# Norm borders of a fused transformer kernel: last tile in token halves, matmuls of the high parts first, one combined sum for the double norm

## The chip, the cores and the metric

The kernel runs on one core of one Trainium2 chip, as one program without collectives. The metric is the device time of an execution in microseconds; the median of several executions is given. About 0.3% (6 us) is what such a measurement can tell from no change.

## What is computed

One sequence of T = 512 tokens and D = 1024 features passes through two layers of a first block (an HGRN and stick-breaking mixer, then a gated mLSTM-like mixer, each followed by a convolutional gated feed-forward), a norm, one layer of a second block (dilated and top-k sparse attention, then a gated feed-forward) and a last norm. What matters here stands between the stages:

```python
def rmsnorm(x, g):
    return x * lax.rsqrt(jnp.mean(x * x, axis=-1, keepdims=True) + EPS) * g

x = x + gate * (y @ w_out)                       # residual
h = rmsnorm(x, g) * (1.0 + scale) + shift        # input of the next stage
```

`gate`, `scale` and `shift` come from a modulation `silu(c) @ ada_w + ada_b`. Between the blocks x is normed twice: x = rmsnorm(x, final_g), then rmsnorm(x, g_attn) enters the second block. The product of the first norm is also the residual stream of the second block.

## The kernel before

All data is kept features on partitions: X is `[128, 8, 512]`, eight tiles of 128 features by 512 tokens (KT = 8). Weights stream from DRAM in 302 chunks of 128x1024 through two buffers (SyncE issues the DMAs). For precision each chunk is split by GpSimd into a high part (L429) and a low part (L431, `w_lo = raw - w_hi`) of type fp32r, in four slots; the split of chunk n waits until TensorE has finished chunk n-4 (`pe_done`, the tiny operation L428). Activations are split in the same way: ScalarE writes `Hhi`, VectorE writes `Hlo`. A matmul block is then three matmuls of 128x512 in fp32r (`three`, L446 to L449): high by high, weight high by activation low, weight low by activation high. One chunk is one output tile: `tile_chunk` (L451) runs k = 0 to 7 with three matmuls each, 24 in all, into one of four PSUM banks G[0..3].

The stages (PHASES, L63) follow each other: even_in, even_out, ffn0, down0, odd_in, odd_out, ffn1, down1, idx_in, attn_in, attn_out, ffn2, down2. Each engine has its own hand-written program; they meet in counting semaphores. VectorE also works through the 144 chunks of the modulation (L1080), and ScalarE issues a few small loads in its own queue.

The first tiles of a stage that follows a norm are run k by k over two output chunks at once (`first_tiles`, L479; three in odd_out, four in even_in), so that TensorE can begin when the first k is there. It waits for `h_ready`, which VectorE raises when the low part is written.

A **norm border** lies between two stages, at r = 1 (behind even_out), 2 (down0), 3 (odd_out), 4 (down1, the double one), 5 (attn_out) and 6 (down2, the end). Its steps, for the last tile m = 7:

1. VectorE adds the residual from PSUM (`residual`, L1098).
2. ScalarE squares the tile (L1724). The squares of the seven tiles before are already added up in `sq_acc` by VectorE (L1365).
3. TensorE sums both over the features, a product with a column of ones per block of 128 tokens (`partial_sums`, L533; each is a pair of loads and matmuls, 8 for a tile), into `normps`.
4. ScalarE takes the root (L1729, in the double and last border L2046), VectorE the reciprocal (L1114). VectorE has meanwhile made the gain column `acol` (L1133).
5. TensorE spreads the 512 values over all partitions, four blocks of 128 tokens (`token_rows`, L555, L558), into `rstdps`.
6. VectorE scales tile k with gain and root (`scaled`, L1151) into `work`; ScalarE adds the shift and writes `Hhi` (L1738); VectorE writes `Hlo` (`low`, L1158).
7. TensorE starts `first_tiles`.

Between these steps TensorE runs dummy matmuls (`keep_warm`, L528, L531) whose results nobody reads: WARM[0] = 2 before the last tile's sums, 1 behind them (3 in the double border), WARM[2] = 4 behind the broadcast. Each is two passes of 256 columns.

In the double border VectorE and ScalarE make a second square of every tile, times `final_g` (L1903), summed in a second accumulator; after the first reciprocal VectorE computes the mean square of the normed x (L1142 to L1144), ScalarE takes a second root (L2051), VectorE a second reciprocal and a product (L1146, L1147). A second broadcast, of the first norm's root, follows the first tiles (L921). In the last border (`normed_x`, L1344) VectorE scales X itself, tile by tile, and SyncE writes each tile out.

## Time and profile before

| | |
|---|---|
| median of 3 runs | 1991.24 us (1988.09 to 1993.24) |
| profiled execution, its own time | 1991.48 us |
| its span, first to last instruction | 1989.7 us |
| TensorE matmul busy | 1923.1 us (97%) |
| TensorE weight load busy | 1551.2 us (78%) |
| VectorE, ScalarE, GpSimd busy | 1034.7, 451.9, 1184.4 us |
| mean granted TensorE clock | 0.985 of full |
| DMA | 242.23 MB, 122 GB/s mean |
| chain that ended last | 86% TensorE, 7% VectorE, 3% ScalarE |

A matmul's own duration in the profile (392 ns in the mean for 128x512) contains its passage through the array; back to back they start 0.23 us apart, so the busy share counts overlapping work once. Idle time of an engine costs only where another engine waits for it.

### The profile page before, as it was taken

Reading aid. Unit: us, or ns where it says so; the run is one execution under the profiler, and the core shown is the slowest. Engines: PE = TensorE matmul, PEld = TensorE weight load, DVE = VectorE, ACT = ScalarE, POOL = GpSimd, SP = SyncE. Lnnn points to the kernel's source line nnn. Section 1 sums busy time; section 2 is a strip of 40 time slices with the busy share of each in tenths; the row PEclk is TensorE's granted clock in tenths of the full one; section 3 lists DMA queues with packets and bytes.
Section 4 is the critical chain, followed back from the end, with each engine's and each line's share of the span. In section 5 each row is a group of like instructions: output and inputs, shape, how many; then the busy total and the mean of one; then the engine's idle time right before and its main releaser. Section 6 shows DMA issues by size and latency. Waiting matters only on the chain.

```text
span 1989.7 us, 25330 instructions
## 1 busy us (share of the span) xinstructions
PE 1923.1 (97%) x8824; PEld 1551.2 (78%) x8824; DVE 1034.7 (52%) x1529; ACT 451.9 (23%) x774; POOL 1184.4 (60%) x907
## 2 busy tenths in 40 slices
PE   5999999999999999999999999999988899999998
PEld 4787868888888887667788888887766688888886
DVE  7566256666655453466766663233877453323222
ACT  3302342211210022352221211112228421111100
POOL 3743326788887955324688787746540256666773
PEclk7999999999999999999999999999989999999999
DMA  7432223455554422111455553322210023222332
GB/s 305 177 117 75 96 95 106 170 190 192 204 193 174 172 96 85 53 52 55 157 191 193 197 189 117 105 96 85 74 59 17 27 82 104 95 95 95 106 105 74
DMA packets 67375, 242.23 MB, mean 122 GB/s; under 512 B 7498, under 2 KB 7882, under 8 KB 67314
## 3 DMA queue, kind: packets, MB, share of 16 engines
q1 hardware_dynamic: 65536, 237.01, 34.2%
q10 hardware_dynamic: 1778, 4.37, 0.6%
q8 instruction: 43, 0.70, 0.1%
q14 instruction: 18, 0.15, 0.0%
HBM read 239.25 MB, written 2.10 MB: 121 GB/s over the span
## 4 chain that ended last, share of the span: by engine, by line
PE 86%; DVE 7%; ACT 3%; issue 2%; DMA 2%; POOL 1%; DVEq 0%; SPq 0%; ACTq 0%; POOLq 0%
PE gemm L447 23%; PE gemm L448 23%; PE gemm L449 23%; DMA w_raw<-wstream 2%; DVE b_score L1630 1%; PE mix L650 1%; PE gemm L474 1%; PE gemm L476 1%; PE gemm L475 1%; DVE b_top L1625 1%; PE mix L447 1%; PE gemm L1046 1%; PE gemm L803 1%; DVE sq_acc L1365 1%; PE mix L449 1%
## 5 line engine op out<-in xcount | busy, mean ns | idle before, releaser
L431 POOL TENSOR_TENSOR w_lo<-w_raw,w_hi 128x1024 fp32r<-128x1024 f32 x302 | 734.9, 2433 | 25.2
L447 PE MATMUL gemm<-h_hi,w_hi 128*128 128x512 f32 x1616 | 634.0, 392 | 20.8 <-DVE h_lo L1186 14.6
L448 PE MATMUL gemm<-h_lo,w_hi 128*128 128x512 f32 x1616 | 630.1, 390 | 0.0
L449 PE MATMUL gemm<-h_hi,w_lo 128*128 128x512 f32 x1616 | 630.1, 390 | 0.0
L428 POOL TENSOR_TENSOR pool_gate<-pool_gate 128x1 f32<-128x1 f32 x298 | 118.3, 397 | 734.4 <-PE gemm L449 592.8
L447 PEld LDWEIGHTS gemm<-h_hi,w_hi 128*128 128x128 f32 x1616 | 304.2, 188 | 90.2 <-issue 21.8
L429 POOL TENSOR_SCALAR w_hi<-w_raw 128x1024 fp32r<-128x1024 f32 x302 | 344.1, 1139 | 17.5 <-DMA w_raw<-wstream 17.5
L449 PEld LDWEIGHTS gemm<-h_hi,w_lo 128*128 128x128 f32 x1616 | 304.0, 188 | 63.8
L448 PEld LDWEIGHTS gemm<-h_lo,w_hi 128*128 128x128 f32 x1616 | 304.1, 188 | 62.0
L1080 DVE CUSTOM_DVE_ANT_0 ada_raw<-ada_raw,c_act 128x1024 f32<-128x1024 f32 x128 | 216.5, 1707 | 110.1 <-DMA ada_raw<-adastream 110.1
L449 PE MATMUL gemm<-p_hi,w_lo 128*128 128x512 f32 x528 | 205.4, 389 | 0.0
L447 PE MATMUL gemm<-p_hi,w_hi 128*128 128x512 f32 x528 | 205.4, 389 | 0.0
L448 PE MATMUL gemm<-p_lo,w_hi 128*128 128x512 f32 x528 | 205.4, 389 | 0.0
L1098 DVE SCALAR_TENSOR_TENSOR x_res<-gemm,modv,x_res 128x512 f32<-128x512 f32 x48 | 35.9, 747 | 238.7 <-PE gemm L449 238.7
L1393 DVE TENSOR_TENSOR work<-work,gemm 128x512 f32<-128x512 f32 x66 | 45.4, 688 | 176.5 <-PE gemm L449 140.3
L1395 DVE TENSOR_TENSOR p_lo<-work,p_hi 128x512 f32 x66 | 98.6, 1494 | 61.4 <-ACT p_hi L1927 61.4
L1724 ACT ACTIVATE sq_tile<-x_res 128x512 f32 x48 | 30.3, 632 | 430.4 <-DVE x_res L1098 430.4
L1365 DVE TENSOR_TENSOR sq_acc<-sq_acc,sq_tile 128x512 f32<-128x512 f32 x42 | 98.6, 2348 | 36.7 <-ACT sq_tile L1724 36.7
L449 PEld LDWEIGHTS gemm<-p_hi,w_lo 128*128 128x128 f32 x528 | 99.1, 188 | 20.8
L448 PEld LDWEIGHTS gemm<-p_lo,w_hi 128*128 128x128 f32 x528 | 99.1, 188 | 20.6
L447 PEld LDWEIGHTS gemm<-p_hi,w_hi 128*128 128x128 f32 x528 | 99.1, 188 | 20.4
L1921 ACT ACTIVATE work<-work 128x512 f32<-128x512 f32 x44 | 27.8, 633 | 307.1 <-DVE work L1388 307.1
(339 smaller groups left out, 1972.0 us busy)
## 6 DMA issues: line engine op xcount, KB each, us to landing
w_raw<-wstream SPq DMA_DIRECT2D x302, 512.0 KB, 3.5
ada_raw<-adastream SPq DMA_DIRECT2D x128, 512.0 KB, 4.3
a_early<-adastream SPq DMA_DIRECT2D x8, 1024.0 KB, 11.9
out<-x_res SPq DMA_DIRECT2D x8, 256.0 KB, 2.2
c_act<-c_in ACTq DMA_DIRECT2D x2, 512.0 KB, 7.2
x_res<-x_in SPq DMA_DIRECT2D x2, 512.0 KB, 6.3
x_res<-x_in ACTq DMA_DIRECT2D x2, 512.0 KB, 9.0
b_dist<-const_in ACTq DMA_DIRECT2D x1, 512.0 KB
```

What stands on the lines that cost most here:

```text
L428: pool.tensor_tensor(pgate[:], pgate[:], pgate[:], ALU.mult)
L429: pool.tensor_scalar(whi[s][:], raw[:, u % RAW, :], 1.0, 0.0, ALU.mult, ALU.add).then_inc(w_hi_done, 1)
L431: pool.tensor_tensor(wlo[s][:], raw[:, u % RAW, :], whi[s][:].bitcast(F32), ALU.subtract).then_inc(w_split, 1)
L447: pe.matmul(out_ap, w_h, r_h, start=first, stop=False)
L448: pe.matmul(out_ap, w_h, r_l, start=False, stop=False)
L449: return pe.matmul(out_ap, w_l, r_h, start=False, stop=last)
L1080: dve.tensor_tensor_reduce(w, w, c, 1.0, start, ALU.mult, ALU.add, total).then_inc(ada_used, 1)
L1098: dve.scalar_tensor_tensor(out=X[:, ds(m, 1), :].rearrange("p a t -> p (a t)"), in0=G[bank][:], scalar=modv[:, ds(gate + m, 1)], in1=X[:, ...
L1365: dve.tensor_tensor(sqacc[:], sqacc[:], sqt[:, m % 2, :], ALU.add).then_inc(sq_added, 1)
L1393: dve.tensor_tensor(work[:, 2 + jj, :], y, G[2 * jj + 1][:], ALU.mult).then_inc(gfree[2 * jj + 1], 1)
L1395: dve.tensor_tensor(Plo[:, ds(2 * i + jj, 1), :].rearrange("p a t -> p (a t)"), work[:, 2 + jj, :], Phi[:, ds(2 * i + jj, 1), :].rearrange ...
L1724: act.activation(sqt[:, slot, :], X[:, ds(m, 1), :].rearrange("p a t -> p (a t)"), ACT.Square).then_inc(sq_ready, 1)
```

## The change

- `first_tiles` waits for the high part of k only, runs the two matmuls of each output tile that use it, and then the low matmuls of k-1; the low matmuls of k = 7 come last. It is used in all nine stages of FILL (L348).
- The last residual, its square and its column sums are made in two halves of 256 tokens. The first two blocks of the root are broadcast into M[0], then blocks 2, 3, 0, 1 into `rstdps` (12 instructions instead of 8); the first tile of `work` and of `Hhi` is made in two halves, the first from M[0].
- The dummies are WARM[0] = 1 before the last sums, WARM[1] = 2 behind them, WARM[2] = 3 behind the broadcast (into M[1]; none in the double border).
- The double norm uses one sum: for gain g the squares are taken with the scale sqrt(g*g + eps) and the root with the bias eps*eps, so that the reciprocal is the product of both norms' factors. The plain sum of the last tile comes behind the broadcast, its root and reciprocal behind the last low part.
- `squares` on ScalarE is unrolled instead of a loop. Columns of `acol` hold the new gains and eps*eps; four semaphores are new (`last_half`, `sq_half`, `bc_half`, `t_half`). No tile is added.

The diff, indented less, without those names, `HALF = T // 2` and some context:

```diff
@@ -74,7 +74,7 @@
...
 ADA_SLOTS = 4
-WARM = (2, 4, 4, 14)
+WARM = (1, 2, 3, 14)
@@ -478,20 +485,31 @@
     def first_tiles(phase, fill, count=2, before={}):
+        def low(k):
+            pe.wait_ge(h_ready, KT * fill + k + 1)
+            for u in range(count):
+                s = (N0[phase] + u) % SPL
+                mm = pe.matmul(G[u][:], whi[s][:, k * P:(k + 1) * P], Hlo[:, k, :], start=False, stop=(k == KT - 1))
+                if k == KT - 1:
+                    mm.then_inc(pe_done, 1)
         for u in range(count):
...
                 before[k]()
-            pe.wait_ge(h_ready, KT * fill + k + 1)
+            w = slice(k * P, (k + 1) * P)
+            pe.wait_ge(hhi_ready, KT * fill + k + 1)
             for u in range(count):
...
                 s = (N0[phase] + u) % SPL
-                mm = three(G[u][:], whi[s][:, k * P:(k + 1) * P], wlo[s][:, k * P:(k + 1) * P],
-                           Hhi[:, k, :], Hlo[:, k, :], k == 0, k == KT - 1)
-                if k == KT - 1:
-                    mm.then_inc(pe_done, 1)
+                pe.matmul(G[u][:], whi[s][:, w], Hhi[:, k, :], start=(k == 0), stop=False)
+                pe.matmul(G[u][:], wlo[s][:, w], Hhi[:, k, :], start=False, stop=False)
+            if k:
+                low(k - 1)
+        low(KT - 1)
     def tiles(phase, bodies, done=0, wide=2):
@@ -525,36 +543,43 @@
...
-    def keep_warm(n):
+    def keep_warm(n, bank=M[0]):
         for _ in range(n):
-            pe.matmul(M[0][:, 0:256], const("ones"), cst[:, 0:256], start=True, stop=True)
-    def partial_sums(c0, tile, first, last):
-        for j in range(NTB):
+            pe.matmul(bank[:, 0:256], const("ones"), cst[:, 0:256], start=True, stop=True)
+    borders = [0]
+    def partial_sums(c0, tile, first, last, blocks=range(NTB)):
+        for j in blocks:
             mm = pe.matmul(normps[:, c0 + j:c0 + j + 1], tile[:, j * P:(j + 1) * P], const("ones")[:, 0:1],
...
     def norm_scale(r):
+        borders[0] += 1
         pe.wait_ge(sq_added, KT * r + KT - 1)
         partial_sums(0, sqacc, True, False)
-        keep_warm(WARM[0])
-        pe.wait_ge(sq_ready, KT * (r + 1))
-        mm = partial_sums(0, sqt[:, 1, :], False, True)
+        c0, last = 0, sqt[:, 1, :]
         if r == 4:
             pe.wait_ge(gsq_added, KT)
-            partial_sums(4, work[:, 2, :], False, False)
+            c0, last = 8, work[:, 1, :]
+            partial_sums(c0, work[:, 2, :], False, False)
+        keep_warm(WARM[0])
+        pe.wait_ge(sq_half, borders[0])
+        partial_sums(c0, last, False, True, (0, 1))
+        if r == 4:
             pe.wait_ge(gsq_ready, KT)
-            mm = partial_sums(4, work[:, 1, :], False, True)
-        mm.then_inc(norm_sum, 1)
-        keep_warm(3 if r == 4 else 1)
-    def token_rows(ps, c0):
-        for j in range(NTB):
+        else:
+            pe.wait_ge(sq_ready, KT * (r + 1))
+        partial_sums(c0, last, False, True, (2, 3)).then_inc(norm_sum, 1)
+        keep_warm(WARM[1])
+    def token_rows(ps, c0, blocks=range(NTB)):
+        for j in blocks:
             mm = pe.matmul(ps[:, j * P:(j + 1) * P], rst[:, c0 + j:c0 + j + 1].broadcast_to([P, P]), const("ident"),
@@ -567,10 +592,16 @@
     def norm(r):
         norm_scale(r)
+        c0 = 8 if r == 4 else 0
         bc[0] += 1
-        bcast(rstdps, bc[0])
-        if r not in (0, 6):
-            keep_warm(WARM[2])
+        pe.wait_ge(rstd_ready, bc[0])
+        token_rows(M[0], c0, (0, 1)).then_inc(bc_half, 1)
+        token_rows(rstdps, c0, (2, 3, 0, 1)).then_inc(rstd_bc, 1)
+        if r == 4:
+            pe.wait_ge(sq_ready, KT * (r + 1))
+            partial_sums(0, sqt[:, 1, :], False, True).then_inc(norm_sum, 1)
+        elif r != 6:
+            keep_warm(WARM[2], M[1])
@@ -583,7 +614,7 @@
...
     bcast(rstdps, bc[0])
-    keep_warm(WARM[2])
+    keep_warm(4)
     def stick_z(h):
@@ -910,11 +941,7 @@
...
-    norm_scale(4)
-    bc[0] += 1
-    bcast(rstdps, bc[0] + 1, 8)
-    keep_warm(WARM[2])
+    norm(4)
     first_tiles("idx_in", FILL["idx_in"])
@@ -1098,15 +1125,12 @@
...
-    def add_square(r, m, slot, first):
-        dve.wait_ge(sq_ready, m + KT * r + 1)
-        if first:
-            ins = dve.tensor_copy(sqacc[:], sqt[:, slot, :])
-        else:
-            dve.wait_ge(sq_added, m + KT * r)
-            ins = dve.tensor_tensor(sqacc[:], sqacc[:], sqt[:, slot, :], ALU.add)
-        ins.then_inc(sq_added, 1)
+    def last_residual(n, m, bank, gate):
+        dve.wait_ge(pe_done, n + 1)
+        for half, done in ((slice(0, HALF), last_half), (slice(HALF, T), gfree[bank])):
+            dve.scalar_tensor_tensor(out=X[:, m, half], in0=G[bank][:, half], scalar=modv[:, gate + m:gate + m + 1],
+                                     in1=X[:, m, half], op0=ALU.mult, op1=ALU.add).then_inc(done, 1)
     def inverse_rms(n, src):
@@ -1124,32 +1148,29 @@
...
     rms_n = [0]
+    borders = [0]
+    def border_inverses(c0):
+        borders[0] += 1
+        rms_n[0] += 1
+        dve.wait_ge(rms_ready, rms_n[0])
+        ready(dve.reciprocal(rst[:, c0:c0 + 4], rms[:, c0:c0 + 4]))
+        dve.wait_ge(bc_half, borders[0])
     def norm(r, fill, g, shift_scale, first_gain=None):
-        rms_n[0] += 1
         a = acol[:, 8 * r:8 * r + 8]
...
                                       op0=ALU.add, op1=ALU.mult))
-        if first_gain is None:
-            ready(inverse_rms(4, rms_n[0]))
-        else:
-            ready(inverse_rms(4, rms_n[0]))
-            dve.wait_ge(rstd_ready, inverses_done[0])
-            rms_n[0] += 1
+        if first_gain is not None:
             link(dve.tensor_tensor(a, a, first_gain, ALU.mult))
-            link(dve.tensor_tensor(rst[:, 4:8], rst[:, 0:4], rst[:, 0:4], ALU.mult))
-            dve.tensor_tensor(rst[:, 4:8], rst[:, 4:8], normps[:, 4:8], ALU.mult).then_inc(sig("second_mean"), 1)
-            dve.wait_ge(rms_ready, rms_n[0])
-            link(dve.reciprocal(rst[:, 8:12], rms[:, 8:12]))
-            ready(dve.tensor_tensor(rst[:, 8:12], rst[:, 8:12], rst[:, 0:4], ALU.mult))
-        spread()
-        def scaled(k):
-            dve.scalar_tensor_tensor(out=work[:, k % 4, :], in0=X[:, k, :], scalar=a[:, k:k + 1], in1=rstdps[:],
-                                     op0=ALU.mult, op1=ALU.mult).then_inc(t_ready, 1)
+        border_inverses(0 if first_gain is None else 8)
+        def scaled(k, part=slice(0, T), done=t_ready, bank=rstdps):
+            dve.scalar_tensor_tensor(out=work[:, k % 4, part], in0=X[:, k, part], scalar=a[:, k:k + 1], in1=bank[:, part],
+                                     op0=ALU.mult, op1=ALU.mult).then_inc(done, 1)
         def low(k):
@@ -1158,18 +1179,24 @@
...
-        scaled(0)
+        scaled(0, slice(0, HALF), t_half, M[0])
+        spread()
+        scaled(0, slice(HALF, T))
         scaled(1)
...
                 scaled(k + 2)
+        if first_gain is not None:
+            rms_n[0] += 1
+            ready(inverse_rms(4, rms_n[0]))
...
     dve.memset(sqacc[:], 1.0).then_inc(sig("ones_set"), 1)
+    dve.memset(eps_sq, EPS * EPS).then_inc(sig("eps_sq_set"), 1)
     dve.memset(modsum[:], 0.0).then_inc(mod_added, 1)
     def first_modulation(k):
@@ -1344,20 +1371,24 @@
     def normed_x(r, g, bank=rstdps, done=False):
         if not done:
-            rms_n[0] += 1
-            ready(inverse_rms(4, rms_n[0]))
+            border_inverses(0)
+            dve.scalar_tensor_tensor(out=X[:, 0, 0:HALF], in0=X[:, 0, 0:HALF], scalar=g[:, 0:1], in1=M[0][:, 0:HALF],
+                                     op0=ALU.mult, op1=ALU.mult)
         spread()
-        for k in range(KT):
+        if not done:
+            dve.scalar_tensor_tensor(out=X[:, 0, HALF:T], in0=X[:, 0, HALF:T], scalar=g[:, 0:1], in1=bank[:, HALF:T],
+                                     op0=ALU.mult, op1=ALU.mult).then_inc(sig("x_normed"), 1)
+        for k in range(0 if done else 1, KT):
             dve.scalar_tensor_tensor(out=X[:, k, :], in0=X[:, k, :], scalar=g[:, k:k + 1], in1=bank[:],
...
     def residual_tiles(phase, r, gate):
         dve.wait_ge(mod_added, gate // 4 - 1)
-        for m in range(KT):
+        for m in range(KT - 1):
             residual(N0[phase] + m, m, m % 4, gate)
-            if m < KT - 1:
-                add_square_prev(r, m)
+            add_square_prev(r, m)
+        last_residual(N0[phase] + KT - 1, KT - 1, 3, gate)
     def add_square_prev(r, m):
@@ -1409,9 +1440,11 @@
...
             for m in range(4):
-                residual(12 * i + N0[phase] + 3 * m + 2, 4 * i + m, m, gate)
                 if 4 * i + m < KT - 1:
+                    residual(12 * i + N0[phase] + 3 * m + 2, 4 * i + m, m, gate)
                     add_square_prev(r, 4 * i + m)
+                else:
+                    last_residual(12 * i + N0[phase] + 3 * m + 2, 4 * i + m, m, gate)
                 if group is not None and 1 <= 4 * i + m <= 4:
@@ -1719,20 +1752,26 @@
...
     scaled = [0]
-    def square(m, slot):
-        act.activation(sqt[:, slot, :], X[:, ds(m, 1), :].rearrange("p a t -> p (a t)"), ACT.Square).then_inc(sq_ready, 1)
-    def norm(r, fill, shift, table=None):
+    borders = [0]
+    def roots(c0, bias):
         nrm[0] += 1
         act.wait_ge(norm_sum, nrm[0])
-        act.activation(rms[:, 0:4], normps[:, 0:4], ACT.Sqrt, bias=col("eps"), scale=1.0 / D).then_inc(rms_ready, 1)
+        act.activation(rms[:, c0:c0 + 4], normps[:, c0:c0 + 4], ACT.Sqrt, bias=bias, scale=1.0 / D).then_inc(rms_ready, 1)
+    def norm(r, fill, shift, table=None):
+        roots(0, col("eps"))
         if table is not None:
...
     def high_tiles(shift):
-        for k in range(KT):
+        act.wait_ge(t_half, borders[0])
+        act.activation(Hhi[:, 0, 0:HALF], work[:, 0, 0:HALF], ACT.Identity, bias=modv[:, shift:shift + 1])
+        act.wait_ge(t_ready, scaled[0] + 1)
+        act.activation(Hhi[:, 0, HALF:T], work[:, 0, HALF:T], ACT.Identity, bias=modv[:, shift:shift + 1]).then_inc(hhi_ready, 1)
+        for k in range(1, KT):
@@ -1892,16 +1931,29 @@
     def squares(r, phase, gain=None):
         act.preload_act_table(ACT.Sqrt)
-        with act.Fori(0, 2) as i:
-            for u in range(4):
-                act.wait_ge(gfree[u], i + G0[phase][u] + 1)
-                act.wait_ge(sq_added, 4 * i + KT * r + u - 1)
-                square(4 * i + u, u % 2)
-                if gain is not None:
-                    act.wait_ge(gsq_added, 4 * i + u + 1)
-                    act.activation(work[:, u % 2, :], X[:, ds(4 * i + u, 1), :].rearrange("p a t -> p (a t)"), ACT.Square,
-                                   scale=cols[:, ds(4 * i + gain + u, 1)]).then_inc(gsq_ready, 1)
+        if gain is not None:
+            link(act.activation(gain, col("final_g", 0, 8), ACT.Square))
+            link(act.activation(gain, gain, ACT.Sqrt, bias=col("eps")))
+        for m in range(KT - 1):
+            act.wait_ge(gfree[m % 4], m // 4 + G0[phase][m % 4] + 1)
+            act.wait_ge(sq_added, KT * r + m - 1)
+            act.activation(sqt[:, m % 2, :], X[:, m, :], ACT.Square).then_inc(sq_ready, 1)
+            if gain is not None:
+                act.wait_ge(gsq_added, m + 1)
+                act.activation(work[:, m % 2, :], X[:, m, :], ACT.Square, scale=gain[:, m:m + 1]).then_inc(gsq_ready, 1)
+        m = KT - 1
+        borders[0] += 1
+        act.wait_ge(sq_added, KT * r + m - 1)
+        if gain is not None:
+            act.wait_ge(gsq_added, m + 1)
+        for half, there, count, done in ((slice(0, HALF), last_half, borders[0], sq_half),
+                                         (slice(HALF, T), gfree[3], G0[phase][3] + 2, sq_ready if gain is None else gsq_ready)):
+            act.wait_ge(there, count)
+            if gain is None:
+                act.activation(sqt[:, 1, half], X[:, m, half], ACT.Square).then_inc(done, 1)
+            else:
+                act.activation(work[:, 1, half], X[:, m, half], ACT.Square, scale=gain[:, m:m + 1]).then_inc(done, 1)
@@ -2033,23 +2085,18 @@
...
     ffn("ffn1", 1, COL["fconv_w"] + 66, COL["fconv_b"] + 22)
-    squares(4, "down1", COL["final_g"])
+    squares(4, "down1", double_gain)
...
-    def root():
-        nrm[0] += 1
-        act.wait_ge(norm_sum, nrm[0])
-        act.activation(rms[:, 0:4], normps[:, 0:4], ACT.Sqrt, bias=col("eps"), scale=1.0 / D).then_inc(rms_ready, 1)
-    root()
-    act.wait_ge(sig("second_mean"), 1)
-    act.activation(rms[:, 8:12], rst[:, 4:8], ACT.Sqrt, bias=col("eps"), scale=1.0 / D).then_inc(rms_ready, 1)
+    act.wait_ge(sig("eps_sq_set"), 1)
+    roots(8, eps_sq)
+    act.activation(sqt[:, 1, :], X[:, KT - 1, :], ACT.Square).then_inc(sq_ready, 1)
     high_tiles(96)
+    roots(0, col("eps"))
@@ -2145,7 +2192,7 @@
...
     squares(6, "down2")
-    root()
+    roots(0, col("eps"))
     return nc
```

## Rows read from the trace of the kernel before

**Rows 1.** The page, part 1: busy us, share of the span, instructions.

```profile
PE 1923.1 (97%) x8824; PEld 1551.2 (78%) x8824; DVE 1034.7 (52%) x1529; ACT 451.9 (23%) x774; POOL 1184.4 (60%) x907
```

**Rows 2.** Timeline, first border: start us, us, engine, line, operation, tiles, count, idle before.

```profile
335.86 0.40 PE L449 MATMUL gemm<-h_hi,w_lo 128*128 128x512 f32 x1
336.29 0.75 DVE L1098 SCALAR_TENSOR_TENSOR x_res<-gemm,modv,x_res 128x512 f32<-128x512 f32 x1 [1.17 <-PE gemm L449]
337.25 0.63 ACT L1724 ACTIVATE sq_tile<-x_res 128x512 f32 x1 [4.82 <-DVE x_res L1098]
337.93 1.05 PE L536 MATMUL mix<-cst,sq_tile 128*128 128x1 f32 x8
339.62 1.16 PE L558 MATMUL mix<-cst,rstd 128*128 128x128 f32 x8
340.61 1.89 PE L531 MATMUL mix<-cst 128*128 128x256 f32 x8
340.82 1.41 DVE L1151 SCALAR_TENSOR_TENSOR work<-x_res,acol,mix 128x512 f32<-128x512 f32 x2 [1.25 <-PE mix L558]
342.35 0.75 DVE L1158 SCALAR_TENSOR_TENSOR h_lo<-work,modv,h_hi 128x512 fp32r<-128x512 f32 x1
343.39 0.47 PE L447 MATMUL gemm<-h_hi,w_hi 128*128 128x512 f32 x1 [0.88 <-DVE h_lo L1158]
343.68 0.74 DVE L1158 SCALAR_TENSOR_TENSOR h_lo<-work,modv,h_hi 128x512 fp32r<-128x512 f32 x1
344.86 0.40 PE L447 MATMUL gemm<-h_hi,w_hi 128*128 128x512 f32 x1
```

**Rows 3.** Timeline, VectorE's small operations beside GpSimd and alone.

```profile
336.55 1.05 POOL L429 TENSOR_SCALAR w_hi<-w_raw 128x1024 fp32r<-128x1024 f32 x1
336.96 0.65 DVE L1133 SCALAR_TENSOR_TENSOR acol<-modv,cols 128x8 f32<-128x8 f32 x1
...
1325.75 0.17 DVE L1142 TENSOR_TENSOR acol<-acol,cols 128x8 f32<-128x8 f32 x1
```

**Rows 4.** Timeline, second border, ScalarE and its queue (ACTq).

```profile
703.88 0.33 ACTq L1933 DMA_DIRECT2D o_gwf<-gatew_in  x1
704.91 0.36 ACTq L1935 DMA_DIRECT2D o_selcol<-const_in  x1
705.49 0.27 ACT L1729 ACTIVATE rms<-mix,cols 128x4 f32<-128x4 f32 x1 [1.14 <-PE mix L536]
```

**Rows 5.** Timeline, VectorE in odd_out and at the third border.

```profile
924.81 0.75 DVE L1098 SCALAR_TENSOR_TENSOR x_res<-gemm,modv,x_res 128x512 f32<-128x512 f32 x1 [0.97 <-PE gemm L449]
...
951.05 2.57 DVE L1365 TENSOR_TENSOR sq_acc<-sq_acc,sq_tile 128x512 f32<-128x512 f32 x1 [0.87 <-ACT sq_tile L1724]
```

**Rows 6.** Timeline, double border.

```profile
1319.77 0.40 PE L449 MATMUL gemm<-p_hi,w_lo 128*128 128x512 f32 x1
1321.60 2.35 POOL L431 TENSOR_TENSOR w_lo<-w_raw,w_hi 128x1024 fp32r<-128x1024 f32 x1
1322.75 2.39 PE L536 MATMUL mix<-cst,work 128*128 128x1 f32 x16
1332.19 0.47 PE L447 MATMUL gemm<-h_hi,w_hi 128*128 128x512 f32 x1 [0.17 <-issue]
```

**Rows 7.** Busy us per engine (double border); granted clock, DMA share, GB/s last.

```profile
1325.00:1330.00 5.00, 5.00 (x17) 4.37 (x18) 1.36 (x7) 0.56 (x2) 0.00 (x0) 0.50 0.63 229
```

**Rows 8.** Timeline, kernel start, first block of even_in.

```profile
35.61 0.76 PE L447 MATMUL gemm<-h_hi,w_hi 128*128 128x512 f32 x1 [12.62 <-DVE h_lo L1186]
40.44 0.48 PE L449 MATMUL gemm<-h_hi,w_lo 128*128 128x512 f32 x1
...
54.43 0.50 PE L447 MATMUL gemm<-h_hi,w_hi 128*128 128x512 f32 x1 [0.79 <-DVE h_lo L1186]
54.71 0.63 ACT L1766 ACTIVATE h_hi<-work 128x512 fp32r<-128x512 f32 x1
...
64.67 0.50 PE L447 MATMUL gemm<-h_hi,w_hi 128*128 128x512 f32 x1 [1.75 <-POOL w_lo L431]
```

7 lines of the change are left out of this document (added).

## The prediction, made before the changed kernel ran

> **What bounds it now.** I read the page first: TensorE is busy for 97% of the span [rows 1], so only what shortens its gaps, or its small products, shows in the time. The chain of waits leads through the matmuls of the helper `three` and leaves them at the norm borders, so I read those in the timeline. At the first border [rows 2] the last matmul ends at 336.26 us and the next comes at 343.39: 7.1 us in which TensorE does tiny products while the tile passes from VectorE (residual) to ScalarE (square), TensorE (sums), ScalarE (root), VectorE (reciprocal), TensorE (broadcast), VectorE (scale), ScalarE (high part) and VectorE (low part). All is serial: each step begins 0.04 to 0.3 us after the one before. The other borders repeat it, the double one takes longer. All times below are from the profiled execution, 1991.48 us for a span of 1989.7; it lies 0.24 us above the median of the runs, which I neglect.
>
> **An ordinary border.** The edit cuts it in four places [rows 2].
> - Residual and square in halves. No row has a half tile. A whole residual takes 0.75 us and a 128x8 operation of VectorE 0.17 [rows 3], so a half is bounded by 0.17 and 0.75; cost grows with elements, so I take the middle, 0.46, the second starting 0.37 after the first. A half on ScalarE, between the root's 0.27 [rows 4] and the square's 0.63, is 0.45. The last half square then ends at 336.29+0.37+0.46+0.21+0.45=337.78 (before 337.88): 0.1 gained.
> - Four of the eight sum instructions (1.05 us for eight) have run by then: 0.5 gained. The root, 0.04 behind the sums, is at 338.42 instead of 339.02.
> - The broadcast grows from 8 instructions to 12; 8 hold VectorE from 339.62 to 340.82, so 12 take 0.5 longer and end at 340.72 instead of 340.22. What hides this is the first half tile, taken from the first two blocks. VectorE's second half ends at 341.18, ScalarE's at 341.70.
> - TensorE starts on the high part alone. Before it waited for the low part too (342.35 to 343.10) and started 0.29 later. Now 341.70+0.29=341.99 instead of 343.39: 1.4 us gained.
>
> Does the supply hold after that? VectorE yields a low part every 1.33 us, TensorE uses one in about 1.4 [rows 2], and high parts come one low part ahead; the second high tile is ready at about 342.7, TensorE wants it at 342.95. It holds with 0.2 to spare. The dummies ahead of the sums fall from two to one, one is added behind the sums, and one is taken from behind the broadcast; the last group (four take 1.89, so three 1.4) would begin at 340.5 and end at 341.9, just ahead of need.
>
> The first two chunks now finish 0.46 us closer together at the end of their block (two matmuls of 0.23 behind the first's last instead of four). GpSimd's next split and the first eviction start that much later, behind which TensorE has two more chunks of 24 matmuls: I cost it at nothing. No DMA is added.
>
> **Borders that get less.** At the second border ScalarE's queue issues three DMAs between the last square and the root, from 703.88 to 705.27 [rows 4]. They now start behind the second half square, about 0.1 later, and the root can't be earlier than 705.4 against 705.49 before: of the 0.6 gained up to the root about 0.05 is left, and the border gains 0.85. At the third (behind odd_out) VectorE never idles from its first residual at 924.81 to the last square sum, which ends at 953.62 [rows 5], after TensorE's last matmul. That stage starts three chunks wide, and the first of them now has two instead of six matmuls behind its last one: the whole row of residuals moves 4x0.23=0.9 us back. Less 0.15 for sums and dummy that queue ahead of the half sums, the border gains 1.4-0.9-0.15=0.35.
>
> **The double border** [rows 6]. Before: last matmul ends 1320.17, next 1332.19, 12.0 us. Removed are one root, two products, one reciprocal and a wait between the engines; eight sum instructions move behind the broadcast. Now TensorE's own order decides: loads of eight sums from 1319.77, eight for the gained squares, one dummy, eight for the last tile, at the 0.12 per load that the first border shows, come to 1323.1; root at 1323.2 to 1323.5. The three DMAs in ScalarE's queue end before that (1.4 us from about 1321.4). VectorE's small gain product now comes when GpSimd's w_lo runs, 1321.60 to 1323.95. At the first border such a 128x8 operation with two SBUF operands took 0.65 instead of 0.17, ending with GpSimd's w_hi [rows 2, 3], so I let it wait: reciprocal at 1324.0 to 1324.2, twelve broadcast instructions, second half tile at 1326.4, ScalarE 1326.9, TensorE 1327.15. The eight moved sums (1.0) end at 1326.7, before that. Gain 5.0 us; without that wait 5.6.
> The Trainium skill (SBUF — State Buffer, section on the two separate sides) calls the pair shared by VectorE and GpSimd an exclusive lock: by it, the wait is real whenever GpSimd is first; if VectorE is first, the sum would be 0.6 better.
>
> **Kernel start.** The first block of even_in uses the same `first_tiles`, four wide. In it TensorE waits for low parts at every k ([rows 8]: 0.79 idle at 54.43 for the sixth), though the high part of the eighth is there at 55.34. Before, 36 matmuls, 0.23 apart, run from 54.43 to 62.7, and the first chunk is done with the 27th, at 60.9; the fifth chunk's split starts only then, and TensorE waits for it until 64.67. Now 4 low matmuls from 54.4, 8 high of k=7 from 55.6, 4 low of k=6, and the first chunk is done at about 58.75. The fifth chunk comes 2.15 us earlier, behind it TensorE is dense until the mixer. I take 2.1; if the mixer isn't waiting for TensorE, 0.
>
> **The end.** The sixth norm border gains 0.6 up to the root, loses 0.5 to the broadcast, and its eight scalings, 0.66 apart (two take 1.41), have half a tile less behind the wait, 0.3: together 0.4 less a hop, 0.35.
>
> **Sum.** 2.1 + 1.4 (first) + 0.85 + 0.35 + 5.0 + 1.4 (behind attn_out) + 0.35 = 11.45 us: 1991.48-11.45 = 1980.0.
>
> **Rivals.**
> (a) The clock eats the gain at the start. TensorE ends that block at 59.3 and would idle 3.2 us until 62.5. Rows show it at full clock after 1.75 us idle at 64.67, and at half after longer waiting: 11 matmuls from 35.61 to 40.44 at 0.43 instead of 0.23 [rows 8], 2.3 us. If this comes back, 1980.0+2.3 = 1982.3; where the mixer doesn't pass the gain, 1982.1. For: the gap nearly doubles; against: it stays below the waits that precede the half-clock rows. Chance 0.15.
> The Trainium skill (TensorE: Matmul & The Clock Gate, Part 1) says that the throttled state is the default and idling brings it back; by that rule this longer gap is the place that speaks against the change, with the same 2.3 us.
> (b) The double border falls to half clock again. There the clock was 0.50 from 1325 to 1330 [rows 7], after sums of one column; the new order is as sparse until 1323.1, with one dummy instead of two. Broadcast and moved sums then take some 1.2 us more and the first ten gemm matmuls 0.2 each: 3.2 us, 1983.2. Chance 0.14.
> (c) Halves cost nearly whole tiles. At 0.75 instead of 0.46 for each, the last residual ends 0.6 later and everything gained in front is gone; only the low part's wait (0.75) is left, less 0.5 of broadcast and 0.2: next to nothing at the four ordinary borders and the last (4.35 lost), and 1 less at the double one: about 1985.4. Against: the 0.17 row. Chance 0.04.
> (d) Slower. In every ordinary border the new order puts one dummy fewer between the last gemm matmul and the last sums. If the clock, full there now (products of one column at 0.12 each [rows 2]), falls at each of them as in the double one, a border pays about 3 us in half-speed broadcast and first matmuls, against 1.4 or less gained. Six borders, 18 us: 1998. It decides from 2.9 us per border on (11.45+6 over six). Against: two dummies and four more broadcast instructions follow right behind the sums, and the double border fell only after 24 sum instructions in a row. Chance 0.03.
> (e) The borders gain nothing because TensorE, once started early, waits for the low parts: VectorE's 1.33 per tile against 1.4 is a thin margin. A loss of 0.2 per tile would undo 1.4 in the eight tiles of a block; the four ordinary borders (4.0 gained) stand as before, 1984.0. Chance 0.06.
>
> **How the numbers follow.** The forecast has 0.58. All cases but (d), with the run-to-run spread of 5 us of the runs before (1988.09 to 1993.24), lie in 1976.5 to 1986: low end if the broadcast wait, GpSimd's lock and TensorE's restart each cost less than taken (2 us) and the median falls well, high end (c). 0.3% of 1991 us is 6 us, about what a measurement can tell from no change; so faster means below 1985.3. The forecast, (a), (b) and most of (e) lie there, (c) stands at the bound: faster 0.91, same 0.06, slower 0.03.
>
> **What would show it.** Right: the next gemm matmul 5.7 us after the last at the first border, 7 us at the double one and without a stretch at 0.50; the root at the second border no earlier relative to the last matmul; the odd_out residuals about 0.9 later; GpSimd's fifth split at about 59; fp32 half tiles of about 0.46. Wrong: half-clock stretches after 59 or at an ordinary border, gaps inside the first blocks while TensorE waits for low parts, or an even_in gain that has vanished by the first border.

## The result, and the profile after

Median 1980.96 us (1977.69 to 1983.79, 5 runs) against 1991.24 (1988.09 to 1993.24, 5 runs) for the kernel before beside them: ratio 0.9948, 95% interval 0.9937 to 0.996. That is 10.3 us; forecast were 11.45, and a time of 1980.0. In a second group, beside 15 executions of the kernel before, the same kernel had a ratio of 0.9956 (first experiment below), which is 8.8 us. The profiled execution is the longest of the five, 1983.79 us with a span of 1982.0, so the traces show only 7.7 us of gain. The first page row answers to [rows 1]:

```profile
PE 1920.2 (97%) x8828; PEld 1552.0 (78%) x8828; DVE 1044.0 (53%) x1539; ACT 454.0 (23%) x787; POOL 1182.5 (60%) x907
```

TensorE's busy time hardly moves: what went is gaps. The timeline of the changed kernel at the first border answers to [rows 2]:

```profile
336.44 0.40 PE L456 MATMUL gemm<-h_hi,w_lo 128*128 128x512 f32 x1
336.87 0.88 DVE L1132 SCALAR_TENSOR_TENSOR x_res<-gemm,modv,x_res 128x256 f32<-128x256 f32 x2 [1.17 <-PE gemm L456]
337.45 0.75 ACT L1954 ACTIVATE sq_tile<-x_res 128x256 f32<-128x256 f32 x2 [4.60 <-DVE x_res L1132]
337.99 0.98 PE L556 MATMUL mix<-cst,sq_tile 128*128 128x1 f32 x8
339.01 0.26 ACT L1761 ACTIVATE rms<-mix,cols 128x4 f32<-128x4 f32 x1 [0.81 <-PE mix L556]
339.78 1.50 PE L583 MATMUL mix<-cst,rstd 128*128 128x128 f32 x12
340.43 0.48 DVE L1172 SCALAR_TENSOR_TENSOR work<-x_res,acol,mix 128x256 f32<-128x256 f32 x1 [0.87 <-PE mix L583]
341.83 0.51 ACT L1773 ACTIVATE h_hi<-work,modv 128x256 fp32r<-128x256 f32 x1 [0.38 <-DVE work L1172]
342.60 0.47 PE L508 MATMUL gemm<-h_hi,w_hi 128*128 128x512 f32 x1
```

The last gemm matmul ends at 336.84, the next starts at 342.60: 5.76 us instead of 7.13. In the rows from top to bottom: the two half residuals together end 0.91 after the last matmul, the root starts 2.17 after it (2.76 before), and TensorE starts on the high part alone, while `h_lo` is only begun at 342.38. A half tile costs 0.48 on VectorE and 0.51 on ScalarE.

The same two ends, read at every border in the profiled execution of the kernel before, of the changed one, and of a second one of the changed kernel (first experiment below):

| us | before | changed | changed, again | forecast gain |
|---|---|---|---|---|
| last gemm matmul before border 1 ends | 336.26 | 336.84 | 333.77 | 2.1 |
| gap, border 1 | 7.13 | 5.76 | 5.77 | 1.4 |
| gap, border 2 | 7.10 | 5.89 | 5.90 | 0.85 |
| gap, border 3 | 7.58 | 7.26 | 5.76 | 0.35 |
| gap, double border | 12.02 | 8.27 | 6.62 | 5.0 |
| gap, border 5 | 7.10 | 5.76 | 5.77 | 1.4 |
| from the last gemm matmul to the end of the span | 12.48 | 12.21 | 12.20 | 0.35 |
| span | 1989.7 | 1982.0 | 1977.5 | |

Three rows differ between the two executions of one kernel, by 3.1, 1.5 and 1.65 us. Two of them, the start and the double border, are TensorE's clock. The 12.02 us of the kernel before contain a fall too: its clock was at 0.50 from 1324.0 to 1330.8 (0.51 in the mean of 1324 to 1331, TensorE busy throughout), so what this row gains is in part the clock's. Busy time by stretch (columns as in [rows 7]) in the first profiled execution of the changed kernel:

```profile
62.00:68.00 6.00, 5.68 (x13) 4.52 (x14) 0.82 (x1) 0.00 (x0) 5.65 (x7) 0.50 0.65 210
1321.00:1325.00 4.00, 4.00 (x20) 3.76 (x19) 0.79 (x3) 1.27 (x3) 0.65 (x1) 0.57 0.92 330
```

and in the second:

```profile
62.00:68.00 6.00, 5.72 (x25) 4.77 (x26) 0.58 (x1) 0.00 (x0) 5.77 (x7) 1.00 0.65 210
1317.00:1321.00 4.00, 4.00 (x33) 3.78 (x31) 1.35 (x4) 1.47 (x4) 1.73 (x1) 1.00 1.00 334
```

Granted clock 0.50 is 1.2 GHz, 1.00 is 2.4: in the same six microseconds TensorE starts 13 matmuls or 25. At the start it had waited just before that (timeline, changed kernel, first execution):

```profile
58.80 1.04 POOL L436 TENSOR_SCALAR w_hi<-w_raw 128x1024 fp32r<-128x1024 f32 x1
62.32 0.80 PE L454 MATMUL gemm<-h_hi,w_hi 128*128 128x512 f32 x1 [3.08 <-POOL w_lo L438]
```

The fifth split comes 2.3 us earlier than before, as forecast, and TensorE idles 3.08 us instead of the 1.75 of [rows 8]. In the double border it never idles ahead of the fall, which comes at 1321.2: from 1317 to 1321 it is busy for 4.00 of 4.00 us at a granted clock of 1.00 (timeline, same execution):

```profile
1318.52 1.03 PE L556 MATMUL mix<-cst,work 128*128 128x1 f32 x8
1319.27 0.17 DVE L1168 TENSOR_TENSOR acol<-acol,cols 128x8 f32<-128x8 f32 x1
1319.31 2.35 POOL L438 TENSOR_TENSOR w_lo<-w_raw,w_hi 128x1024 fp32r<-128x1024 f32 x1
1319.93 0.95 PE L556 MATMUL mix<-cst,work 128*128 128x1 f32 x8
1322.12 2.71 PE L583 MATMUL mix<-cst,rstd 128*128 128x128 f32 x12
1326.15 0.47 PE L508 MATMUL gemm<-h_hi,w_hi 128*128 128x512 f32 x1 [0.53 <-ACT h_hi L1773]
```

Twelve broadcast instructions take 2.71 there and 1.50 at the first border. VectorE's gain product began 0.04 ahead of GpSimd's `w_lo` and was done in 0.17; the wait that the prediction put there did not happen. At the second border ScalarE's queue is ready almost in time:

```profile
703.90 0.36 ACTq L1987 DMA_DIRECT2D o_selcol<-const_in  x1
704.31 0.26 ACT L1761 ACTIVATE rms<-mix,cols 128x4 f32<-128x4 f32 x1 [1.02 <-PE mix L556]
```

The DMAs had begun at 702.88, between the two half squares; the root starts 2.38 after the last gemm matmul, against 2.17 at the first border.

### The profile page after: what moved, and what is told of

Its sections match the earlier page's. It is cut to its first block, busy times and chain, and to the rows that moved or that the text cites. A ratio compares the mean times of both kernels' runs of the same rounds, so it can differ in the third digit from the quotient of the medians.

```text
span 1982.0 us, 25244 instructions
## 1 busy us (share of the span) xinstructions
PE 1920.2 (97%) x8828; PEld 1552.0 (78%) x8828; DVE 1044.0 (53%) x1539; ACT 454.0 (23%) x787; POOL 1182.5 (60%) x907
## 4 chain that ended last, share of the span: by engine, by line
PE 86%; DVE 7%; ACT 3%; issue 2%; DMA 2%; POOL 1%; DVEq 0%; SPq 0%; ACTq 0%; POOLq 0%
PE gemm L454 21%; PE gemm L455 21%; PE gemm L456 21%; PE gemm L508 2%; PE gemm L509 2%; PE gemm L493 2%; DMA w_raw<-wstream 2%; DVE b_score L1663 1%; PE mix L681 1%; PE gemm L481 1%; PE gemm L483 1%; PE gemm L482 1%; DVE b_top L1658 1%; PE gemm L834 1%; DVE sq_acc L1396 1%
## 5 line engine op out<-in xcount | busy, mean ns | idle before, releaser
L454 PE MATMUL gemm<-h_hi,w_hi 128*128 128x512 f32 x1448 | 568.1, 392 | 3.9 <-POOL w_lo L438 3.1
L455 PE MATMUL gemm<-h_lo,w_hi 128*128 128x512 f32 x1448 | 565.6, 391 | 0.0
L456 PE MATMUL gemm<-h_hi,w_lo 128*128 128x512 f32 x1448 | 565.5, 391 | 0.0
L435 POOL TENSOR_TENSOR pool_gate<-pool_gate 128x1 f32<-128x1 f32 x298 | 111.2, 373 | 729.5 <-PE gemm L456 353.1
L454 PEld LDWEIGHTS gemm<-h_hi,w_hi 128*128 128x128 f32 x1448 | 272.9, 188 | 61.5 <-POOL w_lo L438 3.5
L456 PEld LDWEIGHTS gemm<-h_hi,w_lo 128*128 128x128 f32 x1448 | 272.8, 188 | 56.8
L455 PEld LDWEIGHTS gemm<-h_lo,w_hi 128*128 128x128 f32 x1448 | 272.9, 188 | 56.1
L1107 DVE CUSTOM_DVE_ANT_0 ada_raw<-ada_raw,c_act 128x1024 f32<-128x1024 f32 x128 | 222.9, 1757 | 99.3 <-DMA ada_raw<-adastream 99.3
L1396 DVE TENSOR_TENSOR sq_acc<-sq_acc,sq_tile 128x512 f32<-128x512 f32 x42 | 104.6, 2491 | 29.4 <-ACT sq_tile L1941 29.4
L1941 ACT ACTIVATE sq_tile<-x_res 128x512 f32<-128x512 f32 x42 | 26.6, 633 | 375.0 <-DVE x_res L1125 375.0
```

Of the source, the lines that this page charges most:

```text
L435: pool.tensor_tensor(pgate[:], pgate[:], pgate[:], ALU.mult)
L454: pe.matmul(out_ap, w_h, r_h, start=first, stop=False)
L455: pe.matmul(out_ap, w_h, r_l, start=False, stop=False)
L456: return pe.matmul(out_ap, w_l, r_h, start=False, stop=last)
L1107: dve.tensor_tensor_reduce(w, w, c, 1.0, start, ALU.mult, ALU.add, total).then_inc(ada_used, 1)
L1396: dve.tensor_tensor(sqacc[:], sqacc[:], sqt[:, m % 2, :], ALU.add).then_inc(sq_added, 1)
```

## The experiments

The theory: at full clock the gaps shrink by what the steps say, and what an execution then keeps depends on stretches at half clock, which follow idle time of TensorE or come within rows of one-column products. Rivals: order and halves are worth something else than the gaps show; the place of a fall belongs to the kernel. All of them were timed beside the kernel before, in three groups of one chip each; its medians there were 1988.79 (high parts first, without it, dummies at the start, last k chunk by chunk), 1988.92 and 1989.57 us (without halves, and the last two), so ratios are compared, not times. A ratio and the quotient of the two medians differ by up to 0.0009. For each profiled execution I also added up the time at half clock from the granted clock of stretches of 2 us between 45 us and the last border (twice one minus the clock, times 2 us): 34 us for the kernel before, 34 for the changed one, 31 in its second execution. Where TensorE is the bound, half of it is lost.

**The changed kernel again.**

> The changed kernel, unaltered, so that the other kernels of this call and of the one before can be held against it on one chip. Theory A (the times differ from execution to execution by half-clock stretches that come and go, the gaps at full clock do not): the gaps at the borders that keep their clock are again 5.76, 5.9 and 5.76 us for borders 1, 2 and 5; the half-clock stretches need not be those of the first profiled run; the double border is 6.6 us if its clock stays, 8.3 if it falls. Median 1978 to 1981.5. Theory B (the place of the falls belongs to the kernel): half clock again from 61.7 to 68.5 and at the double border, 8.27.

1979.45 us (1979.27 to 1982.62), ratio 0.9956, interval 0.9943 to 0.997. Gaps at full clock were the same to 0.01 us; the half clock at 62 and in the double border was gone, and two were longer, 10.2 us instead of 6.8: in the mixer behind odd_in and in the attention at 1460. So those at the start and in the double border do not belong to the kernel (theory A). Others nearly do: the one in the mixer is in all nine profiled executions, of eight kernels, that leave the wait of 1.67 us ahead of it empty, and only its length varies (6.8 or 10.2). The third difference, border 3, is not the clock. Timeline of this execution, GpSimd and VectorE in odd_out:

```profile
934.98 0.20 POOL L435 TENSOR_TENSOR pool_gate<-pool_gate 128x1 f32<-128x1 f32 x1 [0.84 <-DMA w_raw<-wstream]
936.06 0.69 DVE L1396 TENSOR_TENSOR sq_acc<-sq_acc,sq_tile 128x512 f32<-128x512 f32 x1 [0.70 <-ACT sq_tile L1941]
936.27 2.74 POOL L438 TENSOR_TENSOR w_lo<-w_raw,w_hi 128x1024 fp32r<-128x1024 f32 x1
940.93 2.73 DVE L1396 TENSOR_TENSOR sq_acc<-sq_acc,sq_tile 128x512 f32<-128x512 f32 x1 [0.70 <-ACT sq_tile L1941]
949.90 0.48 DVE L1132 SCALAR_TENSOR_TENSOR x_res<-gemm,modv,x_res 128x256 f32<-128x256 f32 x1 [2.14 <-PE gemm L456]
```

A square sum with both operands in SBUF takes 0.69 us alone and 2.73 beside GpSimd's `w_lo` of 2.4. In the first execution all seven took 2.71 to 2.76 and VectorE went in step with GpSimd, 4.1 us a tile, until it was late for the last one:

```profile
923.77 0.75 DVE L1125 SCALAR_TENSOR_TENSOR x_res<-gemm,modv,x_res 128x512 f32<-128x512 f32 x1 [2.56 <-PE gemm L493]
949.81 2.71 DVE L1396 TENSOR_TENSOR sq_acc<-sq_acc,sq_tile 128x512 f32<-128x512 f32 x1 [0.70 <-ACT sq_tile L1941]
952.44 0.86 DVE L1132 SCALAR_TENSOR_TENSOR x_res<-gemm,modv,x_res 128x256 f32<-128x256 f32 x2
```

In the second one GpSimd waited 0.84 us for weights, the sum slipped in ahead of its `w_lo` (which then took 2.74 instead of 2.4), and VectorE was ahead from there on: 2.14 idle before the last residual, gap 5.76. The later traces repeat it: the four that have a short sum in odd_out have GpSimd waiting 0.62 to 1.14 us for weights just before it and a gap of 5.76, and in the other six that follow all seven sums take 2.54 to 2.77 and the gap is 5.91 to 10.58. The Trainium skill (SBUF — State Buffer, the section on the two separate sides) calls the port pair of VectorE and GpSimd an exclusive lock; 0.69 against 2.73, and the 2.74 of the `w_lo` that came second, agree.

**High parts first alone**: of the diff only the hunk of `first_tiles`, put into the kernel before.

> The kernel before with the new order inside first_tiles alone (high parts first); norm borders as before, nothing left out. Theory A (each part adds up, and the kernel start gives nothing because the clock falls in the longer idle time of TensorE there): the gap at border 1 shrinks from 7.13 to about 6.4 us (the low part's 0.75 gone), at border 2, 5 and the double one by the same 0.7; border 3 by nothing (0.9 given back at odd_out); the start shows the granted clock at 0.50 somewhere between 59 and 69 us and the first border comes within 0.7 us of before. Sum about -3, 1988. Theory B (the start gains and the fall of the clock in the changed kernel was that run's accident): clock 1.00 from 60 to 70, first border 2 us earlier, 1986. Theory C (TensorE started early waits for low parts): gaps shrink, but the blocks behind them grow by the same, 1991.

1989.48 us (1983.49 to 1990.9), ratio 0.9995, 0.9986 to 1.0004: nothing. Yet the gaps at borders 1, 2 and 5 are 6.32 instead of 7.1, and the double one 10.3. Border 3 grew to 10.47 us, with the clock at 0.57 from 954 to 962, the start had 3.4 us at half clock at 62 to 68 (first border 0.75 earlier only), the mixer behind odd_in 10.2: 41 us at half clock in all, mean clock 0.982 to 0.986 over the twelve executions, half of them below 0.984, where none of the 23 of the kernel before beside them was (0.984 to 0.988). The order gains some 0.8 us at borders 1, 2 and 5 and 1.7 at the double one, and loses 2.9 at the third, where TensorE idled 1.27 for VectorE's last sum and the clock fell at 954.6. This execution is still 1.6 us shorter than the profiled one before; that the clock takes the gain back in the twelve is what their mean clock suggests, not more.

**Without high parts first**: that hunk undone in the changed kernel.

> The changed kernel with the old order inside first_tiles (TensorE waits for the low part at every k); halves, broadcast and combined sum stay, nothing left out. Theory A: start as in the kernel before (clock 1.00, last gemm before border 1 at 336.3), border 1 about 0.6 to 0.7 shorter than before (6.45), border 3 about 6.5 (the residuals of odd_out come 0.9 earlier again), double border 9.0, sum about -8 against before: 1983. Theory B (high parts first is worth 2 us at the start besides the borders): 1985 or more. If the half tiles alone gave nothing, the gap at border 1 would be 7.1.

1987.83 us (1984.25 to 1989.01), ratio 0.9987, 0.9979 to 0.9996: 1.0 us below the kernel before by the medians, 2.6 by the ratio, where 8 were expected, so theory B's side (1985 or more). Gaps 6.55, 6.68, 7.16, 8.77 (in part at half clock) and 6.55; border 3 was expected at 6.5, and all seven sums of odd_out took 2.73 or more. The first border comes at 336.07, as before, so the 2.5 us at the start belong to the order of `first_tiles`. The profiled execution is 4.1 us shorter than the one before.

**Without halves**: in the changed kernel whole tiles again, and eight broadcast instructions.

```diff
-for half, done in ((slice(0, HALF), last_half), (slice(HALF, T), gfree[bank])):
+for half, done in ((slice(0, T), gfree[bank]),):
-token_rows(M[0], c0, (0, 1)).then_inc(bc_half, 1)
-token_rows(rstdps, c0, (2, 3, 0, 1)).then_inc(rstd_bc, 1)
+token_rows(rstdps, c0).then_inc(rstd_bc, 1)
...
```

> The changed kernel with whole tiles again (residual, square, sums, eight broadcast instructions, first scaled tile); high parts first, the combined sum and the dummies stay. Nothing left out. Theory A (the terms add up): border 1 and 5 as in the kernel with high parts first alone, 6.3 us (5.76 with halves: 0.55 from the halves); the double border 7.3 to 7.6 where its clock stays, that is the combined sum alone is worth 3.5 to 4 of the 12.0 before. Median 1982 to 1984. Theory B (the halves are worth more because they also keep TensorE fed and its clock up): half-clock stretches at borders 1, 2, 3 or 5, and 1986 or more.

1986.1 us (1983.06 to 1987.62), ratio 0.9981, 0.9972 to 0.999. Borders 1, 2 and 5 are 6.27, so halves are worth 0.5 each at full clock; the double one is 7.85, against 10.3 with the separate sums (high parts first alone), partly at half clock in both. The time is 5 us from the changed kernel's by ratio, and above the 1982 to 1984 of theory A. It is theory B's time, but B's half-clock stretches at borders 1, 2, 3 or 5 are not there: of the 41 us at half clock 10.2 lie in and behind the double border. What costs the rest stays open. In the medians the parts don't add up (0.05% and 0.13% alone, 0.44% together), though they do in the gaps of border 1: 7.13 less 0.81 less 0.58 is 5.74.

**Dummies in the idle time at the start.**

```diff
-            tiles("even_in", 2, wide=4)
+            first_tiles("even_in", FILL["even_in"], 4)
+            keep_warm(7)
+            with pe.Fori(1, 2) as i:
+                for u in range(4):
+                    tile_chunk(4 * i + N0["even_in"] + u, (N0["even_in"] + u) % SPL, u, i + G0["even_in"][u])
```

> The changed kernel with seven more dummy matmuls behind the first block of even_in, in the 3.1 us in which TensorE waits for the fifth chunk; nothing left out. Theory A (the idle time lets the clock fall, and that eats the gain at the start): granted clock 1.00 from 60 to 70 us in the profiled run, first border 2.3 to 2.9 us earlier than in the profiled run of the changed kernel (last gemm at 334 to 334.5 instead of 336.84), median 1978.5 to 1981 and a smaller spread of the runs. Theory B (the mixer does not wait for TensorE, so nothing is passed on): clock 1.00, but the first border stays at 336 to 337 and the time is that of the changed kernel. Theory C (the clock falls for another reason than idleness): 0.50 still, no change.

1980.54 us (1979.35 to 1983.9), ratio 0.9957, 0.9944 to 0.997. Timeline, and busy time by stretch, at the start and at border 3:

```profile
58.97 3.18 PE L549 MATMUL mix<-cst 128*128 128x256 f32 x14
949.50 1.05 PE L556 MATMUL mix<-cst,sq_acc 128*128 128x1 f32 x8 [1.26 <-DVE sq_acc L1400]
```

```profile
62.00:68.00 6.00, 5.94 (x26) 4.80 (x26) 0.93 (x1) 0.00 (x0) 5.72 (x7) 1.00 0.61 216
952.00:956.00 4.00, 4.00 (x16) 3.64 (x16) 0.36 (x2) 1.55 (x2) 0.93 (x1) 0.50 0.74 269
```

The clock stays at the start, the last gemm matmul before border 1 ends at 332.17, 4.7 us earlier than in the first execution, more than the 2.3 to 2.9 expected because the half clock around 190 was absent too. So the mixer does pass the gain on. But border 3 then took 10.58 us: TensorE idled 1.26, waiting for VectorE's sum behind GpSimd's split, and the clock was down from 950.5 to 957.3. Against 5.76 that cost 4.8 us, of which the late sum alone is 1.5 (7.26 in the changed kernel's first execution) and the clock 3.3. It is what rival (d) feared of an ordinary border, behind other idle time; and the same 1.26 us of idle time stood in the changed kernel's first execution without a fall. The time is that of the changed kernel.

**The last k chunk by chunk.**

```diff
-                for k in range(KT):
+                for k in range(KT - 1):
...
-                low(KT - 1)
+                k = KT - 1
+                w, v = slice(k * P, (k + 1) * P), slice((k - 1) * P, k * P)
+                pe.wait_ge(hhi_ready, KT * fill + KT)
+                for u in range(count):
+                    s = (N0[phase] + u) % SPL
+                    pe.matmul(G[u][:], whi[s][:, w], Hhi[:, k, :], start=False, stop=False)
+                    pe.matmul(G[u][:], wlo[s][:, w], Hhi[:, k, :], start=False, stop=False)
...
+                    pe.matmul(G[u][:], whi[s][:, v], Hlo[:, k - 1, :], start=False, stop=False)
...
+                    pe.matmul(G[u][:], whi[s][:, w], Hlo[:, k, :], start=False, stop=True).then_inc(pe_done, 1)
```

> The changed kernel with the last k of first_tiles run chunk by chunk (high matmuls of k = 7, low of k = 6, low of k = 7 for the first chunk, then for the second, and so on) instead of pass by pass, so that the first chunk of a block is done earlier; nothing left out. Theory A (what the new order gives back, it gives back by finishing the chunks of a block close together): GpSimd's fifth split at the start about 2 us earlier (57 instead of 58.8), TensorE's idle time there 1.2 instead of 3.1 us, clock 1.00; in odd_out the first residual about 1.4 us earlier, border 3 gap 6.4 instead of 7.26, the other borders unchanged or 0.1 shorter. Sum 3 to 5 us below the changed kernel in runs where its clock fell, about 1 below where it did not. Theory B (order within the block is indifferent): within 1 us of the changed kernel, border 3 at 7.2.

1980.5 us (1978.82 to 1983.4), ratio 0.9955, 0.9942 to 0.9968. Timeline, GpSimd's fifth split and the first residual of odd_out:

```profile
57.37 2.04 POOL L436 TENSOR_SCALAR w_hi<-w_raw 128x1024 fp32r<-128x1024 f32 x1
920.60 0.75 DVE L1137 SCALAR_TENSOR_TENSOR x_res<-gemm,modv,x_res 128x512 f32<-128x512 f32 x1 [1.19 <-PE gemm L524]
```

The split began 1.43 us earlier but took 2.04 instead of 1.04, beside a VectorE operation on `ada_raw` and `c_act` (57.28 to 58.50), so TensorE's idle time fell only from 3.08 to 2.38, and half the fall stayed (3.4 us). In odd_out the first residual comes 28.9 us ahead of the last matmul instead of 27.55, 1.36 earlier as expected, and the gap at border 3 is 5.91, although all seven sums took 2.73 or more here: that is the order's doing, 1.35 us. The direction was right; the 3 to 5 us expected did not come, and in the time it is not to be told from the changed kernel (0.9956).

**No dummies at the borders**: `WARM = (0, 0, 0, 14)`.

> The changed kernel with no dummy matmuls at the norm borders (counts 1, 2, 3 all 0; those at the kernel's start stay). Nothing left out. Theory A (the dummies keep TensorE's clock up over a border, idleness there brings half clock): half-clock stretches of 3.4 us or more at most of the six borders, gaps of 6.5 to 8 us with broadcast and first matmuls at half speed, 1.7 to 3.4 us each: 1990 to 1996, slower than the kernel before. Theory B (without dummies the broadcast is no longer held and the clock stays): gaps of 5.6, time 1979. Theory C (it falls only at some borders, by where the gap falls in time): between, 1983 to 1988 with a wide spread.

1988.2 us (1984.91 to 1993.0), ratio 0.9997, 0.9987 to 1.0006: theory C, just above its upper end. Timeline and busy time of the first border:

```profile
338.53 1.95 PE L583 MATMUL mix<-cst,rstd 128*128 128x128 f32 x12 [0.64 <-DVE rstd L1158]
341.79 0.76 PE L508 MATMUL gemm<-h_hi,w_hi 128*128 128x512 f32 x1 [1.32 <-ACT h_hi L1773]
```

```profile
340.00:348.00 8.00, 6.68 (x21) 5.16 (x20) 7.49 (x12) 4.42 (x7) 0.00 (x0) 0.60 0.36 131
```

The gap itself is 6.03, the loss comes behind it: the granted clock is at half from 339.6 to 346.4, 6.4 of these 6.8 us within the stretch shown, and the gemm matmuls run in it. The same stands at borders 3 and 5, not at 2 and not at the double one, which is shorter than in the changed kernel (6.18 against 6.62), with its 24 one-column products and no dummy among them. 51 us at half clock, mean clock 0.978 to 0.982. By the ratios the dummies are worth 8.2 us (0.9997 against 0.9956), nearly the whole gain of the change. The kernel before has dummies at its borders too, so this is what dummies are worth, not what the new counts add; no run tests the counts alone.

**Dummies in four waits**, on top of the last k chunk by chunk: five at the start, and

```diff
+            pe.wait_ge(gfree[0], G0["even_in"][0] + 5)
+            keep_warm(5, G[0])
             level(9)
...
                         pe.wait_ge(gfree[u], G0["odd_out"][u])
+                        if u == 0:
+                            keep_warm(4, G[0])
...
+                    pe.wait_ge(gfree[0], G0["attn_in"][0] + 3)
+                    keep_warm(4, G[0])
                     pe.wait_ge(sig("vb_copied"), 4)
```

> The changed kernel with the last k of first_tiles run chunk by chunk, and with dummy matmuls in four waits of TensorE that half-clock stretches followed in the traces so far: five behind the first block of even_in, five ahead of level 9 (2.6 us idle), four ahead of the first scores of odd_in's mixer (1.7 us idle, behind it 6.8 to 10.2 us at half clock) and four ahead of the first scores of the attention (2.3 us idle). Nothing left out. Theory A (idleness ahead brings the half clock, and it costs half its length where TensorE is the bound): the stretches at 62, 189 and 804 us are gone, worth 1.7 + 1.7 + 3.4 to 5.1; the one at 1442 too, without gain where VectorE bounds the attention; median 1972 to 1975. Theory B (the falls there have another cause, such as what TensorE runs behind the wait, products of 64 rows): the stretch at 804 stays, 1977 or more.

1972.59 us (1970.98 to 1976.47), ratio 0.9914, 0.99 to 0.9927. The mixer behind odd_in, from 800 to 812 us in the second execution of the changed kernel, and its counterpart here:

```profile
800.00:812.00 12.00, 10.86 (x26) 7.32 (x27) 6.04 (x17) 2.25 (x4) 2.39 (x2) 0.57 0.15 49
```

```profile
806.00:812.00 6.00, 6.00 (x26) 4.51 (x25) 5.02 (x14) 0.73 (x1) 0.47 (x2) 1.00 0.09 35
```

The four stretches are gone; this execution (the longest of the five) had others, at 131 and 899 behind 0.76 and 0.97 us idle and in the double border (8.29 us), 24 us in all. The products of 64 rows behind the wait were not the cause; the 1.67 us of idle time ahead of them was. The other traces bear this out: in all nine profiled executions that leave that wait empty (eight kernels) the clock falls behind it, in the four with dummies in it not once.

**The same, with the three DMAs of border 2 behind the norm.**

```diff
-            act.wait_ge(pe_done, N0["odd_in"])
-            act.dma_start(gw_f[:], gatew_in).then_inc(small_loaded, 16)
...
             norm(2, 3, 48, ACT.Silu)
+            act.dma_start(gw_f[:], gatew_in).then_inc(small_loaded, 16)
...
```

> As the kernel with the dummies in four waits, and the three DMAs that ScalarE's queue issues at the second border moved behind that norm. Nothing left out. Theory A (these DMAs hold the root back, now by 0.2 us since they start behind the first half square): the root at border 2 comes 2.17 instead of 2.38 us after the last gemm matmul and the gap is 5.76 as at border 1 instead of 5.9; 0.15 us of 1980 can be seen in the trace alone. Theory B (the root waits for its sums there): gap unchanged at 5.9. My own forecast's price was 0.55.

1971.01 us (1970.25 to 1972.13), ratio 0.9905, 0.989 to 0.992: 0.95% below the kernel before and the best ratio of all; not to be told from the kernel without the DMA edit. The root stands 2.18 behind the last gemm matmul, the gap is 5.77:

```profile
699.05 0.26 ACT L1783 ACTIVATE rms<-mix,cols 128x4 f32<-128x4 f32 x1 [0.81 <-PE mix L568]
```

So these DMAs cost 0.13; border 2 takes 5.89 or 5.90 in the six traces that have new order, halves and these DMAs there, and 5.76 or 5.77 in the three that have them behind the norm. In this execution 13.6 us were left at half clock, 3.4 of them in the double border, which took 8.17.

**The double border: plain sums behind the broadcast**, and **two more dummies between the sums**, each on top of the last kernel.

```diff
                 if r == 4:
                     pe.wait_ge(gsq_added, KT)
                     c0, last = 8, work[:, 1, :]
-                    partial_sums(c0, work[:, 2, :], False, False)
+                    partial_sums(c0, work[:, 2, :], True, False)
...
                 if r == 4:
+                    pe.wait_ge(sq_added, KT * r + KT - 1)
+                    partial_sums(0, sqacc, False, False)
                     pe.wait_ge(sq_ready, KT * (r + 1))
```

```diff
                     c0, last = 8, work[:, 1, :]
+                    keep_warm(2)
                     partial_sums(c0, work[:, 2, :], False, False)
```

> As the kernel with filled waits and moved DMAs; in the double border also the eight sums of sq_acc moved from ahead of the root to behind the broadcast, since TensorE itself is the bound there (half A of the gained square is ready 0.9 us before its sums start). Nothing left out. Theory A (24 one-column sums in a row bring the half clock that was seen there in the profiled run): with 16 the clock stays and the gap is 6.2 to 6.5 us instead of 8.2; the last sums end 0.4 to 0.8 earlier behind the last gemm matmul, sixteen sums of 1.9 us behind the broadcast hold the next gemm matmul back by 0.4. Theory B (the fall does not hang on these eight sums): the gap is 8 us again. Median within 1.5 us of that kernel, 1969.5 to 1971.5.

> As the kernel with filled waits and moved DMAs; in the double border also two more dummy matmuls between the sums of sq_acc and those of the gained squares. Nothing left out. Theory A (the row of one-column sums with only one dummy among them lets the clock fall): full clock over the whole border, the gap 8.2 less 1.6 to 2 for the clock, plus 0.9 for the dummies, so 7.1 to 7.5 us; the time 0.7 to 1 below that kernel in executions where it fell, 0.9 above it where it did not. Theory B (a dummy doesn't change it): half clock again and 9 us, 1971.9.

1972.24 us (1970.22 to 1975.22), ratio 0.9919, 0.9906 to 0.9933, and 1971.88 (1971.0 to 1972.81), ratio 0.9912, 0.9899 to 0.9926. With the sums moved, the border in the profiled execution:

```profile
1313.10 0.95 PE L568 MATMUL mix<-cst,sq_acc 128*128 128x1 f32 x8
1314.81 0.49 PE L508 MATMUL gemm<-h_hi,w_hi 128*128 128x512 f32 x1
```

```profile
1309.00:1315.00 6.00, 6.00 (x48) 5.54 (x48) 3.58 (x9) 3.23 (x7) 3.40 (x3) 1.00 0.85 272
```

Full clock and a gap of 6.11; with two more dummies, full clock too and 7.49. As the changed kernel's own order gave full clock in its second execution (6.62), and the kernel without dummies had it with all 24 sums in a row (6.18), one execution each doesn't show that either edit keeps it: that stays open. With the moved sums the median was expected at 1969.5 to 1971.5 and came at 1972.24. The times can't separate the last four kernels.

## Why the prediction was right, and what was off in it

Faster by more than 0.3% as forecast, the time within 1 us, every step of an ordinary border as worked out. The closeness of the time is in part luck: the five executions of the kernel before that stood beside it have a median 1.7 to 2.5 us above those of the three later groups. By its own steps:

- **Ordinary border, 1.4 us.** Measured 1.37 and 1.34. The halves cost 0.48 and 0.51 against estimates of 0.46 and 0.45, and eight half-and-half sums 0.98. Rival (c), halves as dear as whole tiles, is out, and so is (e): in the first blocks behind borders 1, 2 and 5 TensorE has no gap once it has started; the split of the 1.4 was foreseen too, 0.6 up to the root (0.58 to 0.59 by the rows and the kernel with the old order).
- **Border 2, 0.85.** The step "they now start behind the second half square" was mis-sized: the DMAs began behind the first, and the border gained 1.2. Moving them shows their price: 0.13, not 0.55.
- **Border 3, 0.35.** The 0.9 by which the residuals are moved back came as worked out (27.55 instead of 28.46 us ahead of the last matmul), and 0.32 was gained, but "VectorE never idles" was misread and is not true of the kernel: [rows 5] itself has 0.87 idle ahead of the sum, for ScalarE's square, and in the second execution VectorE waited for TensorE besides and 1.8 was gained. What was missing is why a sum takes 2.57 in [rows 5]; the lock that I used for a 128x8 operation at the double border had its real place here.
- **Double border, 5.0.** At full clock 5.4; the lock did not hold the gain product, as the sentence on 5.6 had it. Not all of the 5.4 is fewer steps: the forecast set new steps at full clock against a border that was partly at half ([rows 7]). With the old double sums the gap was 10.31 in the kernel with high parts first alone, where the clock fell later (1326.7); with the 0.81 of that order it is 0.9 less than 12.02, so at least about 0.9 is the clock (my estimate from these rows). With the clock down 3.75: rival (b), the fall priced at 3.2 and measured at 1.65 (8.27 against 6.62), since the first gemm matmuls were spared.
- **Start, 2.1.** At full clock 2.5. Rival (a) came true in the profiled execution, and its price, 2.3, was 3.1. The case against it, that 3.2 us is less than the idle time ahead of the half-clock rows of the start, does not hold: 1.67 us was enough in the mixer behind odd_in, in the kernel before too (half clock from 808.6). The Trainium skill (TensorE: Matmul & The Clock Gate, Part 1) has the throttled state as the default to which idling returns. The start agrees (3.08 us idle, then 0.50), and so does the mixer; in the double border the granted clock fell while TensorE was busy, and there the measurement decides.
- **The end, 0.35.** Measured 0.27.

The step that failed is the way of counting: I gave the falls of the clock chances as if the kernel either had them or not. Some come and go from execution to execution at the same instructions: behind the 3.08 us at the start in four of five traces, in the double border in seven of thirteen. Others, as in odd_in's mixer, are always there and differ in length. In the first profiled execution of the changed kernel two expected gains (3.1 and 1.65) were missing through them, in the second 1.7 went in odd_in's mixer, and a sum of 13.9 in the gaps left 12.2 in the span. The forecast of 11.45 was close to the median's 10.3 because too small terms (double, start, border 2, border 3) stood against falls that it left out. Rival (d) did not come in this kernel, but what it feared is real: without dummies three of the five borders with matmuls behind them fell and the whole gain was gone, and behind a late VectorE border 3 fell with dummies in place, in two of the kernels. What stays open is why the parts of the change gain so much less alone than together in the medians.

## What to carry to other kernels

Read the granted clock of every stretch behind a wait before pricing a shorter gap: an edit that shortens gaps but leaves TensorE idle for 1 to 3 us somewhere can lose what it gained (the new order alone measured nothing), while dummies in four existing waits were worth nearly as much as the whole change to the borders (0.9955 to 0.9914, against 1 to 0.9956). Two engines that share a port can lock step for a whole stage, so look at one operation's time beside and without the other engine before you call it its cost. And profile twice: the terms of a sum that differ between two executions of one kernel are not the kernel's.

## What the runs showed that I had not expected

- The clock falls with TensorE busy all the time: in the double border of the changed kernel's first execution behind 24 products of one column with one dummy among them, during the two behind (1317.7 to 1321.2), and it is back at 2.4 GHz before the gemm matmuls begin. It did not fall there in the second execution, nor without any dummy, so these products are not enough by themselves.
- A fall after 1.67 us idle, and 6.8 or 10.2 us at half clock behind it although TensorE is then busy without a gap from 801 on.
- The kernel with filled waits and moved DMAs ran with a mean granted clock of 0.990 to 0.991, the kernel before beside it with 0.984 to 0.987; 13.6 us at half clock instead of the 31 of the changed kernel's second execution are 8.7 us if TensorE is the bound in all of them, and by the ratios it beats that kernel by 10 (0.9905 against 0.9956).
- A 128x512 sum on VectorE: 0.69 us alone, 2.73 beside GpSimd's low split, four times the price, and GpSimd's wait of 0.84 us for weights, by chance, ended it.
